# Hybrid S5 and attention trunk: first transfers reordered and merged, ScalarE's input squares and sines moved behind the split of the seventh weight unit

## The chip, the cores and the metric

The kernel runs on one core of a Trainium2 chip. The metric is the device time of one execution in microseconds (us); lower is better. The core has five engines that run side by side and meet through semaphores: TensorE (PE, its weight loads are called PEld), VectorE (DVE), ScalarE (ACT), GpSimd (POOL) and SyncE (SP), which here only issues transfers (DMAs).

## The reference

The input is `x`, 256 tokens of 1024 channels. There are two layers, each of the form

```
h = h + 0.5 * swiglu(rmsnorm(h), ffn1)
h = h + mixer(rmsnorm(h))         # layer 0: S5 state space + GLU; layer 1: MoBA attention
h = h + 0.5 * swiglu(rmsnorm(h), ffn2)
```

and a last rmsnorm. `swiglu` multiplies by a 1024 x 5632 matrix, takes silu(g) * u, and multiplies by a 2816 x 1024 matrix. `rmsnorm` needs for each token the mean of its squares; because the gain is folded into the matmul's input, the factor 1/rms of a token (the kernel's `rs`) can be applied to the matmul's result. The S5 mixer needs, for each of 64 groups with 64 states, `exp(a_re*dt)`, `cos(a_im*dt)`, `sin(a_im*dt)` with `dt = exp(log_step)`, and from them matrices built of `b_re`, `b_im`, `c_re`, `c_im` and powers of the decay. All is float32.

## The kernel before, in words

Each float32 matmul is done as three matmuls of rounded parts: hi*hi, lo*hi and hi*lo. So the weights have to be split on the way. A *unit* is 128 x 1024 weights (512 KB). SP loads units in order into six buffers `raw` (`load`, L294). ACT copies one into its rounded high part `w_hi` (`split`, L539 to L546). DVE subtracts to get the low part `w_lo` (L779 to L785). PE then runs twelve 512-column matmuls on it (`unit`, L1108). `w_hi` and `w_lo` have four buffers, so ACT may be four units ahead of PE. Units are counted from 0 here; the seventh is unit 6.

Phase 0 is the first half of the first swiglu: eleven blocks of four units each. Block 0 is units 0 to 3, block 1 is units 4 to 7. Each block fills two PSUM banks (one for 128 tokens each). Then ACT applies silu with the scale `rs` (`gate`, L555), DVE multiplies by u (`gated`, L813, tile `prod`), and PE transposes `prod` (`turn_hidden`, L1055). PE has the transposes of block b-1 in its program behind the second unit of block b: for block 0 they stand behind unit 5 and ahead of unit 6, and they wait for DVE's `drained`. ACT's `gate` of block 0 waits for `rs_ready`, which POOL raises once it has the mean squares (`inverse_rms`, L363, waits for `sq_done`).

Every engine works through its own program in order. ACT's program at the start is: the rounded input `x_hi` in eight tiles, with the splits of units 0 to 2 in between (L650 to L660); the exponential of `log_step` (L662); four squares of the input `h` with a sum each (L664 to L671), which wait for the two transfers of `h`; then `dense(0)`, whose loop splits unit j+3 at step j of block 0, and behind the split at j = 1 (unit 4) does the S5 angles (`s5_angles`, L637: one Exp, two Sin); at the next block it does `gate` of block 0 and goes on with the split of unit 7.

SP's program is at first: `xt` in four parts with units 0 to 3 in turn; the two halves of `h`; `skip`, `b_re`, `b_im`, `c_re`, `c_im`; then all other units from 4 on. From unit 6 on a load waits until the buffer is free (L297). ACT issues the small transfers: `gains`, `a_re`, `a_im`, and `log_step` in two.

POOL prepares the S5 tables meanwhile (L387 to L465): it computes the angle, waits for the squares (L403), for `b` and `c` (L404), and for ACT's three angle results (L409), and then works through a long chain of small operations on `sm`, `w2`, `cp`, `rotc` and `rots`. It needs to be done when PE has finished phase 1, since its next work (`w2_bd`, L477, the first step of the S5 mixer) waits for that (L468).

Of the kernel before, what the change touches and what calls it, by code (L numbers as in the profile page):

```python
# [12 lines left out]
ACT = mybir.ActivationFunctionType  # L13
# [4 lines left out]
P = 128  # L18
TOK = 256
TT = TOK // P  # L20
D = 1024
DT = D // P
# [9 lines left out]
S5_G, S5_J, S5_N = 64, 16, 64  # L32
GP = S5_G // 2
# [5 lines left out]
NB = 512  # L39
# [3 lines left out]
RAW = 6  # L43
# [51 lines left out]
def trunk(nc, io, out):  # L95
    phases = plan()
    units = [(p, v) for p in phases for v in range(p.units)]
# [4 lines left out]
    def sb(name, shape, dt=F32, where=None):  # L102
        return (where or ctx).enter_context(nc.sbuf_tensor(name, shape, dt))

    def sem(name):
        return ctx.enter_context(nc.semaphore(name))

    with ctx:
# [5 lines left out]
        h = sb("h", [P, TT, D])  # L114
        prod = sb("prod", [P, 2, TT, HB])
        act_out = sb("act_out", [P, TT, HB])
        ident = sb("ident", [P, P])
        gains = sb("gains", [P, 7, DT])
        skip = sb("skip", [P, DT])
        half = sb("half", [P, 2])  # L120
        nhalf = sb("nhalf", [P, 2])
        eye = sb("eye", [P, 32])
        ss = sb("ss", [P, TT, 4])
# [29 lines left out]
        with ExitStack() as area:  # L153
            w2 = sb("w2", [P, 2, STEP, GP, S5_J], F32, area)
# [3 lines left out]
            sm = sb("sm", [P, SMALLS, GP], F32, area)  # L158
            u = sb("u", [P, DT, TOK], F32, area)
            with ExitStack() as inner:  # L160
                tmp = sb("tmp", [P, 4, GP * S5_J], F32, inner)
# [4 lines left out]
            states = sb("states", [P, 2, PPT, 2, CH], F32, area)  # L166
# [42 lines left out]
        h_in = [sem(f"h_in{q}") for q in range(TT)]  # L209
        par_in = sem("par_in")  # L210
        s5_a_in = sem("s5_a_in")
        s5_in = sem("s5_in")
        consts = sem("consts")
        warm = sem("warm")
        low_first = sem("low_first")
        high_first = sem("high_first")
        sq_done = sem("sq_done")
# [74 lines left out]
        @block.sync  # L292
        def _(sp):
            def load(gu):  # L294
                p, v = units[gu]
                if gu >= RAW:
                    sp.wait_ge(lo_done, gu - RAW + 1)  # L297
                b, j = divmod(v, p.upb)
                if gu == 0:
                    for i in range(KU):  # L300
                        cols = slice(NB * i, NB * i + NB)
                        sp.dma_start(raw[:, 0, cols], io[WEIGHTS[p.n]][b, :, cols])\
                          .then_inc(first_in[i], 16)
                    return
                sp.dma_start(raw[:, gu % RAW, :], io[WEIGHTS[p.n]][b, :, j * UW:j * UW + UW])\
                  .then_inc(landed[gu % RAW], 16)

            for c in range(DT // 2):
                sp.dma_start(xt[:, 2 * c:2 * c + 2, :], io["xt"][:, 2 * c:2 * c + 2, :])\
                  .then_inc(x_in[c], 16)  # L310
                load(c)
            for q in range(TT):
                sp.dma_start(h[:, q, :], io["x"][q, :, :]).then_inc(h_in[q], 16)
            sp.dma_start(skip[:, :], io["skip"]).then_inc(s5_in, 16)
            for r, name in ((0, "b_re"), (1, "b_im")):
                sp.dma_start(tmp[:, r, :], io[name]).then_inc(s5_in, 16)
            for r, name in ((0, "c_re"), (1, "c_im")):
                sp.dma_start(w2[:, r, 0, :, :].rearrange("p g j -> p (g j)"), io[name])\
                  .then_inc(s5_in, 16)
            for gu in range(DT // 2, len(units)):  # L320
                load(gu)
            for q in range(TT):
                for ready, cols in ((left_ready, slice(0, NB)), (right_ready, slice(NB, D))):
                    sp.wait_ge(ready, q + 1)
                    sp.dma_start(out[q, :, cols], fin[:, q, cols]).then_inc(out_sent, 16)
            sp.wait_ge(out_sent, 16 * 2 * TT)

        @block.gpsimd
        def _(pool):
# [30 lines left out]
            def ts(o, a, s1, s2, op0=ALU.mult, op1=ALU.add):  # L360
                link(pool.tensor_scalar(o, a, s1, s2, op0, op1))
# [13 lines left out]
            def s(i):  # L375
                return sm[:, i, :]
# [7 lines left out]
                tt(o_i, t1, t2, ALU.add)  # L384

            ts(nhalf[:, :], half[:, :], -1.0, 0.0)
            pool.wait_ge(s5_a_in, 16 * 4)  # L387
            ts(s(A_RE), s(A_RE), -1e-4, 0.0, ALU.min, ALU.add)
            pool.wait_ge(s5_exp, 1)
            tt(s(XA), s(A_RE), s(DTM), ALU.mult)  # L390
# [10 lines left out]
            pool.tensor_scalar(s(RR), s(RR), PI_LOW, -PI_LOW, ALU.min, ALU.max)\  # L401
                .then_inc(s5_small, 1)
            inverse_rms(None)  # L403
            pool.wait_ge(s5_in, 16 * 5)  # L404

            for r in range(2):
                link(pool.tensor_scalar(cp[:, r, :, 0, :],
# [61 lines left out]
            for d in range(DT):  # L469
                b = d % 2  # L470
# [54 lines left out]

        @block.scalar
        def _(act):
            act.dma_start(gains[:, :, :], io["gains"]).then_inc(par_in, 16)
            act.wait_ge(consts, 1)
            act.activation(act_out[:, 0, 0:TT], mhalf[:, :], ACT.Copy).then_inc(warm, 1)  # L530
            act.dma_start(sm[:, 0, :], io["a_re"]).then_inc(s5_a_in, 16)
            act.dma_start(sm[:, 1, :], io["a_im"]).then_inc(s5_a_in, 16)
            for g in range(2):
                act.dma_start(sm[64 * g:64 * g + 64, 2, :],
                              io["log_step"][g:g + 1, :].broadcast_to([64, GP])).then_inc(s5_a_in, 16)

            tally = {"sq": 2 * TT}

# [86 lines left out]
            def dense(n, chained=True):  # L625
                p = phases[n]
                for b in range(p.blocks):
                    for j in range(p.upb):
                        if b:
                            after(p, b - 1, j)  # L630
                        elif chained:
                            after(phases[n - 1], phases[n - 1].blocks - 1, j)
                        split(p.unit0 + b * p.upb + j + LEAD)
                        if n == 0 and b == 0 and j == 1:
                            s5_angles()

            def s5_angles():  # L637
                act.wait_ge(s5_small, 1)
                act.activation(sm[:, 9, :], sm[:, 4, :], ACT.Exp).then_inc(s5_exp, 1)
                act.activation(sm[:, 10, :], sm[:, 7, :], ACT.Sin).then_inc(s5_exp, 1)  # L640
                act.activation(sm[:, 11, :], sm[:, 7, :], ACT.Sin, scale=0.5).then_inc(s5_exp, 1)
# [8 lines left out]
            for d in range(DT):  # L650
# [7 lines left out]
                    split(1)  # L658
                if d == 5:
                    split(2)  # L660
            act.wait_ge(s5_a_in, 16 * 4)
            act.activation(sm[:, 3, :], sm[:, 2, :], ACT.Exp).then_inc(s5_exp, 1)  # L662
            act.wait_ge(warm, 1)
            for q in range(TT):  # L664
                act.wait_ge(h_in[q], 16)
                for c in range(2):
                    if q or c:
                        act.wait_ge(sq_done, 2 * q + c)
                    act.activation(act_out[:, :, :].rearrange("p q x -> p (q x)"),  # L669
                                   h[:, q, NB * c:NB * c + NB], ACT.Square,  # L670
                                   accum_out=ss[:, q, c:c + 1]).then_inc(sq_done, 1)  # L671
            dense(0, False)
            dense(1)
            squares(phases[1], 1, NB)

# [708 lines left out]
```

## Time and profile before

| what | us |
|---|---|
| median of 3 timed runs (lowest, highest) | 1003.34 (1002.96, 1005.39) |
| profiled execution | 1005.62 |
| its span, first to last instruction | 1003.8 |
| PE busy | 976.4 (97%) |
| DVE busy | 596.8 (59%) |
| ACT busy | 485.1 (48%) |
| POOL busy | 238.2 (24%) |

The busy time of an engine leaves out waits, so an engine at 97% is the one that sets the time as long as its idle pieces are not on a path of others. The profile's tables give a start in us from the span's start, a duration, the engine, the line of the kernel and the tile written and read; in brackets stands how long the engine was idle before and what ended it. TensorE's granted clock is shown as a share of full speed: 1.00 is 2.4 GHz and 0.50 is 1.2 GHz.

### The profile page before, as it was taken

To read this page: it belongs to the slowest core of one execution; us is meant where nothing else is said; L and a number is where in the kernel's file an instruction comes from. 1 tells how busy PE (TensorE), PEld (TensorE's weight loads), DVE (VectorE), ACT (ScalarE), POOL (GpSimd) and SP (SyncE) were. 2 spreads that over 40 slices of the span, in tenths; PEclk is the share of its full clock that TensorE was granted. 3 is DMA by queue.
4 is the path that set the end of the run, shared out by engine and by line. 5 is a ranking of instruction groups with operands and counts; after the bars stand their busy time and mean duration, and the time that the engine had idled before them with its cause. 6 is when DMAs were issued, how large, how long until landed. Compare 5 with 4: busy or idle time off the path is not lost.

```text
span 1003.8 us, 14476 instructions
## 1 busy us (share of the span) xinstructions
PE 976.4 (97%) x5754; PEld 808.7 (81%) x5754; DVE 596.8 (59%) x732; ACT 485.1 (48%) x688; POOL 238.2 (24%) x307
## 2 busy tenths in 40 slices
PE   7999999888899999999999999999999999999997
PEld 6888888777788888888888888888887788888886
DVE  4767755859766555554565555554566465555544
ACT  6544444423265544544463444543457464444442
POOL 4999989779300000000000000000050000000000
PEclk9999999959999999999999999999999999999999
DMA  9766666600056566666656666666661256566651
GB/s 339 232 187 187 187 191 182 197 2 4 23 173 191 186 186 188 190 195 185 202 176 188 189 186 183 187 182 195 184 184 62 86 172 187 186 188 189 184 173 42
DMA packets 48035, 169.33 MB, mean 169 GB/s; under 512 B 5984, under 2 KB 5984, under 8 KB 47968
## 3 DMA queue, kind: packets, MB, share of 16 engines
q1 hardware_dynamic: 47232, 167.80, 55.0%
q8 instruction: 46, 0.75, 0.3%
q10 hardware_dynamic: 736, 0.60, 0.2%
q14 instruction: 21, 0.17, 0.1%
HBM read 167.33 MB, written 1.05 MB: 168 GB/s over the span
## 4 chain that ended last, share of the span: by engine, by line
PE 92%; POOL 2%; DVE 2%; issue 1%; ACT 1%; DMA 1%; SPq 0%; POOLq 0%; DVEq 0%; ACTq 0%
PE ps L1053 88%; PE ps L1064 2%; POOL w_bd L477 1%; DMA h<-in_x 1%; PE ps L1077 1%; PE ps L1194 1%; POOL c_bd L488 1%; PE ps L1286 1%; PE ps L1090 0%; PE ps L1258 0%; DVE scan L968 0%; ACT act_out L669 0%; ACT w_hi L545 0%; POOL decay L495 0%; PE ps L1313 0%
## 5 line engine op out<-in xcount | busy, mean ns | idle before, releaser
L783 DVE TENSOR_TENSOR w_lo<-raw,w_hi 128x1024 fp32r<-128x1024 f32 x311 | 406.1, 1309 | 276.3 <-ACT w_hi L545 275.7
L545 ACT ACTIVATE w_hi<-raw 128x1024 fp32r<-128x1024 f32 x311 | 328.4, 1058 | 274.0 <-PE ps L1053 271.7
L1053 PE MATMUL ps<-w_hi,x_hi 128*128 128x512 f32 x896 | 355.6, 397 | 4.3 <-DVE w_lo L783 4.2
L1053 PE MATMUL ps<-w_hi,x_lo 128*128 128x512 f32 x896 | 350.2, 391 | 0.0
L1053 PE MATMUL ps<-w_lo,x_hi 128*128 128x512 f32 x896 | 349.7, 390 | 0.0
L1053 PEld LDWEIGHTS ps<-w_hi,x_hi 128*128 128x128 f32 x896 | 169.0, 189 | 39.5 <-DVE w_lo L783 5.0
L1053 PEld LDWEIGHTS ps<-w_hi,x_lo 128*128 128x128 f32 x896 | 168.7, 188 | 36.1
L1053 PEld LDWEIGHTS ps<-w_lo,x_hi 128*128 128x128 f32 x896 | 169.2, 189 | 33.6
L1053 PE MATMUL ps<-w_hi,hid_hi 128*128 128x512 f32 x352 | 137.6, 391 | 0.0
L1053 PE MATMUL ps<-w_hi,hid_lo 128*128 128x512 f32 x352 | 137.0, 389 | 0.0
L1053 PE MATMUL ps<-w_lo,hid_hi 128*128 128x512 f32 x352 | 137.0, 389 | 0.0
L358 POOL TENSOR_TENSOR ms<-ss 128x2 f32<-128x2 f32 x6 | 1.2, 200 | 536.0 <-ACT act_out L583 535.5
L1053 PEld LDWEIGHTS ps<-w_hi,hid_lo 128*128 128x128 f32 x352 | 66.1, 188 | 13.8
L1053 PEld LDWEIGHTS ps<-w_lo,hid_hi 128*128 128x128 f32 x352 | 66.1, 188 | 13.6
L1053 PEld LDWEIGHTS ps<-w_hi,hid_hi 128*128 128x128 f32 x352 | 66.1, 188 | 13.5
L574 ACT ACTIVATE hid_hi<-ps 128x512 fp32r<-128x512 f32 x44 | 26.3, 599 | 88.0 <-PE ps L1064 88.0
L834 DVE TENSOR_TENSOR hid_lo<-ps,hid_hi 128x512 fp32r<-128x512 f32 x44 | 30.4, 692 | 57.1 <-ACT hid_hi L574 57.1
L565 ACT ACTIVATE act_out<-ps,rs 128x256 f32<-128x256 f32 x88 | 41.5, 475 | 46.2 <-PE ps L1053 46.1
L821 DVE SCALAR_TENSOR_TENSOR prod<-ps,rs,act_out 128x256 f32<-128x256 f32 x88 | 41.8, 480 | 18.0 <-ACT act_out L565 18.0
L523 POOL TENSOR_TENSOR rs<-end_ms,mhalf 128x1 f32<-128x1 f32 x2 | 1.1, 553 | 183.7 <-DVE end_ms L1042 183.7
L358 POOL TENSOR_TENSOR sm<-sm 128x32 f32<-128x32 f32 x64 | 34.3, 535 | 10.5 <-ACT sm L662 3.9
L358 POOL TENSOR_TENSOR tmp<-cp,sm 128x512 f32<-128x512 f32 x16 | 26.7, 1666 | 1.3
(129 smaller groups left out, 664.6 us busy)
## 6 DMA issues: line engine op xcount, KB each, us to landing
raw<-in_in SPq DMA_DIRECT2D x175, 512.0 KB, 4.1
raw<-in_out SPq DMA_DIRECT2D x88, 512.0 KB, 3.6
raw<-in_glu SPq DMA_DIRECT2D x16, 512.0 KB, 3.8
raw<-in_k SPq DMA_DIRECT2D x8, 512.0 KB, 4.5
raw<-in_v SPq DMA_DIRECT2D x8, 512.0 KB, 4.4
raw<-in_q SPq DMA_DIRECT2D x8, 512.0 KB, 4.3
raw<-in_o SPq DMA_DIRECT2D x8, 512.0 KB, 4.1
xt<-in_xt SPq DMA_DIRECT2D x4, 256.0 KB, 6.1
```

The source lines that it names most:

```text
L358: link(pool.tensor_tensor(o, a, b, op))
L477: pool.tensor_scalar(w2_bd[:, b, r, :, :, cols], w2[:, r, :, PPT * d:PPT * d + PPT, :], half[:, g:g + 1], 0.0, ALU.mult, ALU.add).then_inc ...
L488: pool.tensor_scalar(c_bd[:, d % 3, r, :, :, cols], cp[:, r, PPT * d:PPT * d + PPT, :, :], (half, nhalf)[r][:, g:g + 1], 0.0, ALU.mult, AL ...
L545: act.activation(w_hi[:, gu % WS, :], raw[:, gu % RAW, :], ACT.Copy)\
L565: act.activation(act_out[:, q, :], ps[:, bank(p.block0 + b, q), 0:HB], ACT.Silu, scale=rs[:, q:q + 1]).then_inc(act_ready, 1)
L574: act.activation(hid_hi[:, 2 * b:2 * b + 2, :].rearrange("p f x -> p (f x)"), ps[:, KT + hb % 2, :], ACT.Copy).then_inc(hid_hi_done, 1)
L783: dve.tensor_tensor(w_lo[:, gu % WS, :], raw[:, gu % RAW, :], w_hi[:, gu % WS, :].bitcast(F32), ALU.subtract)\
L821: dve.scalar_tensor_tensor(prod[:, hb % 2, q, :], ps[:, bank(gb, q), HB:NB], rs[:, q:q + 1], act_out[:, q, :], ALU.mult, ALU.mult).then_in ...
L834: dve.tensor_tensor(hid_lo[:, 2 * b:2 * b + 2, :].rearrange("p f x -> p (f x)"), ps[:, KT + hb % 2, :], hid_hi[:, 2 * b:2 * b + 2, :].rear ...
L1053: return pe.matmul(o, w, x, start=start, stop=stop, skip_group_check=True)
L1064: last = pe.transpose(ps[:, KT + hb % 2, f * TOK + q * P:f * TOK + q * P + P], prod[:, hb % 2, q, f * P:f * P + P], ident[:, :])
L1077: last = pe.transpose(ps[:, TA + t % 2, i * TOK + q * P:i * TOK + q * P + P], h[:, q, d * P:d * P + P], ident[:, :])
```

## The change

SP's order of transfers becomes: `xt` and units 0 to 3 as before, unit 4, the two halves of `h`, unit 5, `b` (both parts in one transfer), `c` (both in one), unit 6 and so on. `skip` travels with `gains` in one transfer on ACT's queue; `a_re`, `a_im` and `log_step` (now repeated for every state in the input) come in one transfer `a_step` in place of four. On ACT the four squares of the input leave their place ahead of `dense(0)` and the angles leave theirs behind the split of unit 4; both now stand behind the split of unit 6, squares first, and so directly ahead of `gate` of block 0.

```diff
-        gains = sb("gains", [P, 7, DT])
-        skip = sb("skip", [P, DT])
+        gains_skip = sb("gains_skip", [P, 8 * DT])
+        gains = gains_skip[:, 0:7 * DT].rearrange("p (n d) -> p n d", d=DT)
+        skip = gains_skip[:, 7 * DT:8 * DT]
...
                 load(c)
+            load(4)
             for q in range(TT):
                 sp.dma_start(h[:, q, :], io["x"][q, :, :]).then_inc(h_in[q], 16)
-            sp.dma_start(skip[:, :], io["skip"]).then_inc(s5_in, 16)
-            for r, name in ((0, "b_re"), (1, "b_im")):
-                sp.dma_start(tmp[:, r, :], io[name]).then_inc(s5_in, 16)
-            for r, name in ((0, "c_re"), (1, "c_im")):
-                sp.dma_start(w2[:, r, 0, :, :].rearrange("p g j -> p (g j)"), io[name])\
-                  .then_inc(s5_in, 16)
-            for gu in range(DT // 2, len(units)):
+            load(5)
+            sp.dma_start(tmp[:, 0:2, :].rearrange("p r x -> p (r x)"), io["b"]).then_inc(s5_in, 16)
+            sp.dma_start(w2[:, :, 0, :, :].rearrange("p r g j -> p r (g j)"),
+                         io["c"].rearrange("p (r x) -> p r x", r=2)).then_inc(s5_in, 16)
+            for gu in range(RAW, len(units)):
                 load(gu)
...
-            act.dma_start(gains[:, :, :], io["gains"]).then_inc(par_in, 16)
+            act.dma_start(gains_skip[:, :], io["gains_skip"]).then_inc(par_in, 16)
             act.wait_ge(consts, 1)
             act.activation(act_out[:, 0, 0:TT], mhalf[:, :], ACT.Copy).then_inc(warm, 1)
-            act.dma_start(sm[:, 0, :], io["a_re"]).then_inc(s5_a_in, 16)
-            act.dma_start(sm[:, 1, :], io["a_im"]).then_inc(s5_a_in, 16)
-            for g in range(2):
-                act.dma_start(sm[64 * g:64 * g + 64, 2, :],
-                              io["log_step"][g:g + 1, :].broadcast_to([64, GP])).then_inc(s5_a_in, 16)
+            act.dma_start(sm[:, 0:3, :].rearrange("p n g -> p (n g)"), io["a_step"]).then_inc(s5_a_in, 16)
...
                         split(p.unit0 + b * p.upb + j + LEAD)
-                        if n == 0 and b == 0 and j == 1:
+                        if n == 0 and b == 0 and j == 3:
+                            input_squares()
                             s5_angles()
+
+            def input_squares():
+                act.wait_ge(warm, 1)
+                for q in range(TT):
+                    act.wait_ge(h_in[q], 16)
+                    for c in range(2):
+                        if q or c:
+                            act.wait_ge(sq_done, 2 * q + c)
+                        act.activation(act_out[:, :, :].rearrange("p q x -> p (q x)"),
+                                       h[:, q, NB * c:NB * c + NB], ACT.Square,
+                                       accum_out=ss[:, q, c:c + 1]).then_inc(sq_done, 1)
...
             act.activation(sm[:, 3, :], sm[:, 2, :], ACT.Exp).then_inc(s5_exp, 1)
-            act.wait_ge(warm, 1)
-            for q in range(TT):
-                act.wait_ge(h_in[q], 16)
-                for c in range(2):
-                    if q or c:
-                        act.wait_ge(sq_done, 2 * q + c)
-                    act.activation(act_out[:, :, :].rearrange("p q x -> p (q x)"),
-                                   h[:, q, NB * c:NB * c + NB], ACT.Square,
-                                   accum_out=ss[:, q, c:c + 1]).then_inc(sq_done, 1)
             dense(0, False)
```

The waits on `s5_a_in` and `s5_in` are lowered to the new numbers of transfers. Nothing that is computed changes.

## Rows read from the trace of the kernel before

**Rows 1.** The page, busy shares and the chain that ended last, by engine:

```profile
PE 976.4 (97%) x5754; PEld 808.7 (81%) x5754; DVE 596.8 (59%) x732; ACT 485.1 (48%) x688; POOL 238.2 (24%) x307
PE 92%; POOL 2%; DVE 2%; issue 1%; ACT 1%; DMA 1%; SPq 0%; POOLq 0%; DVEq 0%; ACTq 0%
```

**Rows 2.** Timeline of PE: start, duration, what, [idle before, releaser]:

```profile
17.10 0.39 PE L1053 MATMUL ps<-w_hi,x_lo 128*128 128x512 f32 x1
19.88 0.50 PE L1053 MATMUL ps<-w_hi,x_hi 128*128 128x512 f32 x1 [2.39 <-DVE w_lo L783]
...
28.19 0.60 PE L1064 MATMUL ps<-ident,prod 128*128 128x128 f32 x4
...
266.87 1.29 PE L1053 MATMUL ps<-u,k_t 32*32 32x256 f32 x32 [3.64 <-DVE k_t L988]
```

**Rows 3.** Timeline of ACT at the start:

```profile
13.08 0.21 ACT L662 ACTIVATE sm<-sm 128x32 f32<-128x32 f32 x1
14.57 0.63 ACT L669 ACTIVATE act_out<-h 128x512 f32<-128x512 f32 x1 [1.27 <-DMA h<-in_x]
...
17.52 1.04 ACT L545 ACTIVATE w_hi<-raw 128x1024 fp32r<-128x1024 f32 x1
19.73 1.06 ACT L545 ACTIVATE w_hi<-raw 128x1024 fp32r<-128x1024 f32 x1 [1.17 <-DMA raw<-in_in]
20.70 0.21 ACT L639 ACTIVATE sm<-sm 128x32 f32<-128x32 f32 x1
20.93 1.28 ACT L640 ACT_TABLE_LOAD   x1
...
22.48 1.99 ACT L545 ACTIVATE w_hi<-raw 128x1024 fp32r<-128x1024 f32 x2
24.49 1.28 ACT L565 ACT_TABLE_LOAD   x1
25.78 0.84 ACT L565 ACTIVATE act_out<-ps,rs 128x256 f32<-128x256 f32 x2
```

**Rows 4.** Timeline of DVE at the start:

```profile
18.60 1.23 DVE L783 TENSOR_TENSOR w_lo<-raw,w_hi 128x1024 fp32r<-128x1024 f32 x1 [4.17 <-ACT w_hi L545]
...
26.29 0.88 DVE L821 SCALAR_TENSOR_TENSOR prod<-ps,rs,act_out 128x256 f32<-128x256 f32 x2 [0.32 <-ACT act_out L565]
```

**Rows 5.** Chain of waits, 0 to 32 us, one piece (start, us):

```profile
5.50 8.98 DMA h<-in_x
```

**Rows 6.** SP's issues of units 3 and 6 (timeline), and their us to landing:

```profile
4.78 0.69 SPq L305 DMA_DIRECT2D raw<-in_in  x1
raw<-in_in SPq DMA_DIRECT2D x1, 512.0 KB, 8.4
11.09 1.07 SPq L305 DMA_DIRECT2D raw<-in_in  x1
raw<-in_in SPq DMA_DIRECT2D x1, 512.0 KB, 11.2
```

**Rows 7.** DMA queues in 0 to 14 us, ACT's queue: packets, MB, share of 16 engines:

```profile
q10 hardware_dynamic: 592, 0.08, 3.5%
```

**Rows 8.** Timeline of POOL:

```profile
18.98 2.02 POOL L407 TENSOR_SCALAR cp<-w 128x512 f32<-128x512 f32 x2
22.71 0.24 POOL L358 TENSOR_TENSOR sm<-sm 128x32 f32<-128x32 f32 x1 [1.71 <-ACT sm L641]
...
187.33 3.27 POOL L358 TENSOR_TENSOR rots<-tmp 128x1024 f32<-128x1024 f32 x1
197.05 1.84 POOL L477 TENSOR_SCALAR w_bd<-w,half 128x256 f32<-128x256 f32 x4 [6.46 <-PE ps L1053]
```

**Rows 9.** Stretches: length, busy PE, PEld, DVE, ACT, POOL, PEclk, DMA, GB/s:

```profile
17.50:19.90 2.40, 0.02 (x1) 0.03 (x1) 1.23 (x1) 1.23 (x4) 2.03 (x4) 1.00 1.03 421
268.00:270.00 2.00, 2.00 (x76) 1.75 (x66) 0.00 (x0) 0.11 (x1) 0.00 (x0) 0.58 0.00 0
270.00:272.00 2.00, 2.00 (x6) 1.57 (x7) 0.72 (x2) 1.64 (x3) 0.00 (x0) 0.57 0.04 8
```

More of the change, by code:

```diff
@@ L386, in _ @@
             ts(nhalf[:, :], half[:, :], -1.0, 0.0)
-            pool.wait_ge(s5_a_in, 16 * 4)
+            pool.wait_ge(s5_a_in, 16)
             ts(s(A_RE), s(A_RE), -1e-4, 0.0, ALU.min, ALU.add)
@@ L403, in _ @@
             inverse_rms(None)
-            pool.wait_ge(s5_in, 16 * 5)
+            pool.wait_ge(s5_in, 16 * 2)
             for r in range(2):
@@ L660, in _ @@
                     split(2)
-            act.wait_ge(s5_a_in, 16 * 4)
+            act.wait_ge(s5_a_in, 16)
             act.activation(sm[:, 3, :], sm[:, 2, :], ACT.Exp).then_inc(s5_exp, 1)
-            act.wait_ge(warm, 1)
-            for q in range(TT):
-                act.wait_ge(h_in[q], 16)
-                for c in range(2):
-                    if q or c:
-                        act.wait_ge(sq_done, 2 * q + c)
-                    act.activation(act_out[:, :, :].rearrange("p q x -> p (q x)"),
-                                   h[:, q, NB * c:NB * c + NB], ACT.Square,
-                                   accum_out=ss[:, q, c:c + 1]).then_inc(sq_done, 1)
             dense(0, False)
@@ L1357 @@
         "xt": _np.ascontiguousarray(x["x"][0].T.reshape(DT, P, TOK).transpose(1, 0, 2)),
-        "gains": tiles(_np.stack([x["ffn1_norm"][0], x["mix_norm"][0], x["ffn2_norm"][0],
-                                  x["kv_norm"], x["ffn1_norm"][1], x["mix_norm"][1],
-                                  x["ffn2_norm"][1]])),
+        "gains_skip": _np.ascontiguousarray(tiles(_np.stack([
+            x["ffn1_norm"][0], x["mix_norm"][0], x["ffn2_norm"][0], x["kv_norm"], x["ffn1_norm"][1],
+            x["mix_norm"][1], x["ffn2_norm"][1], x["s5_d"][0]])).reshape(P, -1)),
         "last_gain": _np.ascontiguousarray(x["final_norm"].reshape(1, D)),
-        "skip": tiles(x["s5_d"][0]),
-        "a_re": states(x["s5_a_re"][0]), "a_im": states(x["s5_a_im"][0]),
-        "log_step": _np.ascontiguousarray(x["s5_log_step"][0].reshape(GP, 2).T),
-        "b_re": states(x["s5_b_re"][0]), "b_im": states(x["s5_b_im"][0]),
-        "c_re": states(x["s5_c_re"][0].transpose(0, 2, 1)),
-        "c_im": states(x["s5_c_im"][0].transpose(0, 2, 1)),
+        "a_step": _np.concatenate([states(x["s5_a_re"][0]), states(x["s5_a_im"][0]),
+                                   states(_np.repeat(x["s5_log_step"][0][:, None], S5_N, 1))], 1),
+        "b": _np.concatenate([states(x["s5_b_re"][0]), states(x["s5_b_im"][0])], 1),
+        "c": _np.concatenate([states(x["s5_c_re"][0].transpose(0, 2, 1)),
+                              states(x["s5_c_im"][0].transpose(0, 2, 1))], 1),
         "glu": stream(x["s5_w_glu"][0], True),
```

## Prediction

> **What bounds the kernel now.** I read the page first. PE is busy 97% of the span and makes up 92% of the chain that ended last [rows 1]. So the question for an edit at the start is only: at what time does PE get through its first units, and does anything behind that give time back or take more? The timeline of PE answers the first half. Unit 2's last matmul starts at 17.10, and matmuls follow each other every 0.227 us, so unit 3 could start at 17.33; it starts at 19.88, 2.55 us later [rows 2]. The brackets name DVE's low part of unit 3, which starts at 18.60 behind ACT's high part at 17.52 [rows 3, 4]. ACT had been free from 13.29 on, but its program put the four squares of the input first, and these waited until 14.57 for the first half of `h` [rows 3]; the chain of waits shows the same transfer, 5.50 to 14.48 [rows 5]. Unit 3 itself had landed at 4.78 + 8.4 = 13.2 [rows 6]. From 19.88 on PE shows no idle time up to the transposes of block 0: units 3, 4 and 5 at 2.73 us each (12 x 0.227) give 28.1, and the transposes stand at 28.19 [rows 2]. They need DVE's `prod`, which was ready at 26.29 + 0.88 = 27.17 [rows 4]: a cover of 1.0 us only. That is the number on which the prediction turns.
>
> The second half is POOL. Its S5 tables end at 187.33 + 3.27 = 190.60, and it then waits 6.46 us for PE to finish phase 1 at about 197.0 [rows 8].
>
> **The change part by part.**
>
> *Squares out of the way of unit 3: a gain at first.* ACT can split unit 3 at 13.3, DVE has its low part before 16, so unit 3 starts at 17.33: PE is 2.55 us early. Unit 4, loaded ahead of `h`, takes the place in which `h` landed (14.5), and is ready before PE's 20.1. Unit 5 comes three transfers of 512 KB later. The rate: from `h` at 14.48 to unit 6 at 11.09 + 11.2 = 22.3 [rows 5, 6] the queue carries six times 512 KB (half of `h`, `b`, `c`, units 4, 5, 6), 1.30 us each. So unit 5 lands at 18.4, is split by 20.8, and PE wants it at 22.8. PE would end unit 5 at 17.33 + 3 x 2.73 = 25.5, against 28.1 before.
>
> *What is late next: the gate of block 0.* The order of transfers ahead of unit 6 changes, their bytes do not, so unit 6 lands at 22.3 again. Before, ACT had done the squares and the angles while it waited for transfers. Now they stand between unit 6's split and the gate. From durations in [rows 3]:
> - split of unit 6 to the next instruction: 0.97 (19.73 to 20.70);
> - four squares: 2.95 (14.57 to 17.52);
> - Exp, table load, two Sin: 1.78 (20.70 to 22.48);
> - table load for silu: 1.29 (24.49 to 25.78);
> - first silu to the end of the second `prod` on DVE: 27.17 - 25.78 = 1.39 [rows 3, 4].
>
> The sum is 8.38, and 0.1 for the semaphore to PE. From 22.3 the transposes of block 0 would start at 30.8. POOL's `rs` is not later than the silu table: 1.46 us behind the squares (17.52 to 18.98 [rows 3, 8]), less than the 3.07 of angles and table load. So PE, through with unit 5 at 25.5, waits over 4.5 us for the transposes, and unit 6 is queued behind them on PE. Instead of 2.55 us early PE is 2.6 us late against 28.19.
>
> *Fewer transfers.* ACT's small transfers took 3.5% of the 16 engines over 14 us, 0.49 us [rows 7]. Of 592 packets some 256 remain, so about 0.3 us is saved, and `skip`'s 128 packets save perhaps 0.1 more at the same rate. Bounds: 0 (they were interleaved with issue gaps) and 1.0 (twice the whole of ACT's queue). I take 0.4: unit 6 at 21.9, transposes at 30.4, PE 2.2 us late. The waits for `s5_a_in` end earlier on POOL, which waits for Exp at 13.08 anyway: nothing.
>
> The Trainium skill has a rule that speaks for this part: "DMA: Bandwidth & Descriptors", Bandwidth, says that transfers under 64 KB are dominated by their descriptors. The trace bounds what that is worth here by the 0.49 us above.
>
> *The clock.* An idle stretch of nearly 5 us (25.5 to 30.4) is new. In this trace PE was idle for 3.64 us up to 266.87 [rows 2], ran on, and from about 268.3 to 271.7 its granted clock was 0.5 (0.58 and 0.57 over two stretches of 2 us): PE lost 0.42 x 2 + 0.43 x 2 = 1.7 us there [rows 9]. The shorter gap at 17.5 to 19.9 kept 1.00 [rows 9]. The new gap is longer than either. Bounds: 0, if the clock stays or falls and rises within the gap, and 3.4, two such stretches. I take 1.4: one stretch of half clock whose first part falls in the idle time.
>
> *POOL.* Its chain started at 22.71 behind ACT's sines. Now: squares end, `rs`, the two copies of 2.02, then the chain. Squares end at 21.9 + 0.97 + 2.95 = 25.8; `rs` and copies +1.46 and +2.1: 29.4. The chain is 6.7 us later and ends at 197.3, if its operations take what they took (I allow +-2). PE ends phase 1 at 197.0 + 2.2 + 1.4 = 200.6. POOL is covered by 3 us, and costs nothing; the cover before was 6.46 [rows 8].
>
> *Behind that.* All later phases follow PE's end of phase 1, so nothing gives the time back. `w_hi` buffers, loads and the gate of block 1 are as before, shifted.
>
> **Sum.** -2.55 (unit 3 earlier) + 4.75 (wait for the transposes, net +2.2) + 1.4 (clock) = +3.6 us. Against the profiled execution (span 1003.8, whole 1005.62) that is 1009.2. The timed runs' median is 2.3 us under the profiled one, so the forecast is 1003.34 + 3.6 = 1006.9. What a measurement can tell from no change is 0.3%, 3.0 us: 1000.3 to 1006.35.
>
> **The rivals.**
> 1. *The clock stays up* (it did over the gap of 2.4 us). Then +2.2: 1005.5, within 0.3%. Against it: three microseconds of idle and more were followed by half clock at 268. Chance 0.17.
> 2. *The other side: the gate is not late.* If unit 6 is at ACT long before 21.9 (by 17.0, were the transfers faster at the start), or ACT gets through the list above inside PE's units 4 and 5, PE keeps 2.55 us and is at the end of phase 1 at 194.5. Then POOL decides: its chain ends at 197.3 when the sines stay where the diff has them, the S5 stage starts at 197.3 in place of 197.05, and the result is +0.3: 1003.6. If POOL's chain has less contention or starts sooner, it lies between that and -2.55, 1000.8; only beyond that is it faster by 0.3%. It decides from the point where `prod` of block 0 is ready by 28.2. For it: nothing but errors in my landing times; against it: unit 6's bytes are the same. Chance 0.15, of which 0.05 is faster than 1000.3.
> 3. *The clock takes two stretches,* or half clock comes again in S5 by another alignment: +2.2 + 3.1 = +5.3, 1008.6. Chance 0.13.
> 4. *Table loads cost more than their row when they stand close together:* ScalarE would have to empty first. In [rows 3] the load of 1.28 starts 0.02 behind the Exp and the silu 0.01 behind its load, so I see no such time; with one more 1.4 us on each of two loads, +2.8 on the forecast: 1009.7. Chance 0.03. The Trainium skill says this ("ScalarE: Activation LUTs", What ACT_TABLE_LOAD costs: a drain of some 1.38 us beside the load of 1.28). The trace agrees on the 1.28 and shows no drain.
>
> The forecast itself has 0.52. Its own spread (unit 6's landing +-0.6, clock 0.7 to 1.7) is 1005.6 to 1007.8.
>
> **How the numbers follow.** Slower than 1006.35: two thirds to three quarters of the forecast (0.38), rivals 3 and 4 (0.15), and a little of rival 1 by the scatter of medians (0.02): 0.55. Faster: 0.06. The rest, 0.39, within 0.3%. The range from 1003.3 (rival 2's +0.3, less a little scatter) to 1009.0 leaves out the faster part of rival 2, rival 4 and half of the tail of 3, together under 0.2.
>
> **What would show it.** Unit 3's first matmul at about 17.3 with no idle time before it: the first gain is right. Unit 4 landed at about 14.5, unit 6 at 21.9. ACT in the order split 6, four squares, Exp, two table loads with the sines between, silu from about 29.0. PE idle for 4 to 5 us ahead of L1064 released by DVE's `prod`: the central step. PEclk under 1 at 30 to 33: the clock term; 1.00 there: rival 1. POOL's idle time before L477 near 3 us; if it is 0, rival 2 or a longer POOL chain. The prediction is wrong if the transposes of block 0 start before 28.2, or if ACT's squares are done before unit 6 is split.

## The result, and the profile after

The change made the kernel slower. Five runs of each gave medians of 1008.95 us (1006.21 to 1012.15) and 1002.96 us (1001.87 to 1005.39) for the kernel before, with a ratio of 1.0064, 95% interval 1.0038 to 1.0090. In a later session twelve runs of the same changed kernel stood against 35 of the kernel before: 1006.47 and 1003.62, ratio 1.0028, interval 1.0010 to 1.0047. By the ends of the two intervals the change costs 1 to 9 us, and the forecast of +3.6 lies in between. The direction and the mechanism were right. One term was too small, the landing of unit 6, and the spread of single runs was larger than I had allowed for. Both are read from the profiles below.

The timeline of PE after the change, the rows that answer to [rows 2]:

```profile
24.69 0.39 PE L1052 MATMUL ps<-w_hi,x_lo 128*128 128x512 f32 x1
32.25 1.12 PE L1063 MATMUL ps<-ident,prod 128*128 128x128 f32 x4 [7.17 <-DVE prod L820]
...
45.05 0.60 PE L1063 MATMUL ps<-ident,prod 128*128 128x128 f32 x4
```

No idle time stands before unit 3 any more: PE is through unit 5 at 25.1, 3 us earlier than before. Then it waits 7.17 us for `prod` of block 0, and the transposes stand at 32.25 in place of 28.19. The next ones follow 12.80 us later; in the kernel before, blocks without a disturbance are 11.36 us apart. The difference of 1.4 us is the clock, which stands at half for a part of it (rows below).

ACT and DVE, answering to [rows 3, 4]:

```profile
13.40 1.04 ACT L541 ACTIVATE w_hi<-raw 128x1024 fp32r<-128x1024 f32 x1
14.69 1.06 ACT L541 ACTIVATE w_hi<-raw 128x1024 fp32r<-128x1024 f32 x1 [0.24 <-DMA raw<-in_in]
18.47 1.06 ACT L541 ACTIVATE w_hi<-raw 128x1024 fp32r<-128x1024 f32 x1 [2.72 <-DMA raw<-in_in]
23.73 1.06 ACT L541 ACTIVATE w_hi<-raw 128x1024 fp32r<-128x1024 f32 x1 [4.20 <-DMA raw<-in_in]
24.70 0.61 ACT L641 ACTIVATE act_out<-h 128x512 f32<-128x512 f32 x1
...
27.63 0.21 ACT L647 ACTIVATE sm<-sm 128x32 f32<-128x32 f32 x1
27.86 1.28 ACT L648 ACT_TABLE_LOAD   x1
...
29.52 1.28 ACT L561 ACT_TABLE_LOAD   x1
30.82 0.84 ACT L561 ACTIVATE act_out<-ps,rs 128x256 f32<-128x256 f32 x2
```

```profile
31.32 0.88 DVE L820 SCALAR_TENSOR_TENSOR prod<-ps,rs,act_out 128x256 f32<-128x256 f32 x2 [5.28 <-ACT act_out L561]
```

ACT stands idle for 2.72 and for 4.20 us while it waits for units 5 and 6, with the four squares and the angles still undone; then it does them ahead of the gate. From unit 6's landing to the transposes it takes 32.25 - 23.75 = 8.50 us; the sum in the prediction had 8.48.

Unit 6 is where the size went wrong. SP's issue and its us to landing, answering to [rows 6]:

```profile
9.05 0.68 SPq L306 DMA_DIRECT2D raw<-in_in  x1
raw<-in_in SPq DMA_DIRECT2D x1, 512.0 KB, 14.7
```

It landed at 9.05 + 14.7 = 23.75. (The view gives the second number to 0.1, so a landing is good to 0.05 us; ACT's split of unit 6 starts at 23.73.) The prediction took 21.9 and bounded it by 21.3 and 22.3. The transfers ahead of it came at its pace of one per 1.3 us: unit 4 at 14.7, the halves of `h` at 15.9 and 17.2, unit 5 at 18.4, `b` at 19.5, `c` at 21.0. One more step of 1.3 would have put unit 6 at 22.3. So the loss lies between `c` and unit 6, and there the DMA view shows a packet of another queue, called instruction, which is not in the same stretch of the kernel before. First the four transfers from unit 5's landing to unit 7's in the changed kernel, then the four behind `c_im` up to unit 7 in the kernel before:

```profile
q1 hardware_dynamic: 807, 2.61, 102.4%
q8 instruction: 1, 0.02, 1.1%
```

```profile
q1 hardware_dynamic: 579, 2.11, 102.5%
```

The packet carries 16 KB and takes one of the 16 DMA engines for 1.1 us, beginning at 21.56. The four transfers took 6.4 us with it and 5.1 without. The queues together moved 411 GB/s in both stretches, which fits one engine's share of a unit that comes late, and not a slower stream. In the kernel before such a packet begins at 25.2, behind unit 6's landing. The section on why the prediction was right or wrong has the other profiles.

The clock (busy us of PE, PEld, DVE, ACT, POOL, then PEclk, DMA share, GB/s), and POOL, answering to [rows 8, 9]:

```profile
28.43:35.26 6.83, 3.01 (x9) 2.57 (x10) 3.50 (x5) 6.51 (x10) 5.93 (x13) 0.50 0.19 53
28.00:32.00 4.00, 0.00 (x0) 0.00 (x0) 0.68 (x2) 3.96 (x7) 3.33 (x9) 0.55 0.27 111
32.00:36.00 4.00, 3.75 (x13) 3.15 (x14) 3.56 (x5) 2.98 (x4) 3.52 (x7) 0.59 0.23 51
```

The clock is at half for 6.83 us. The first 3.8 of them fall in PE's wait, 3.0 behind the transposes, and these cost the 1.4 to 1.5 us.

```profile
202.54 1.86 POOL L477 TENSOR_SCALAR w_bd<-w,half 128x256 f32<-128x256 f32 x4 [4.50 <-PE ps L1052]
```

POOL is still idle for 4.50 us when phase 1 ends (6.46 before), so its later start costs nothing. Phase 1 ends 202.54 - 197.05 = 5.5 us later, and the span is 5.9 us longer (1009.7).

### The profile page after: what moved, and what is told of

Read it like the earlier page. It is cut to its first block, busy times and chain, and to the rows that moved or that the text cites. A ratio compares the mean times of both kernels' runs of the same rounds, so it can differ in the third digit from the quotient of the medians.

```text
span 1009.7 us, 14470 instructions
## 1 busy us (share of the span) xinstructions
PE 978.1 (97%) x5754; PEld 809.6 (80%) x5754; DVE 594.3 (59%) x732; ACT 485.1 (48%) x688; POOL 240.8 (24%) x307
## 4 chain that ended last, share of the span: by engine, by line
PE 91%; DVE 2%; POOL 2%; issue 1%; DMA 1%; ACT 1%; SPq 1%; POOLq 0%; DVEq 0%; ACTq 0%
PE ps L1052 86%; PE ps L1063 2%; DMA raw<-in_in 1%; POOL w_bd L477 1%; PE ps L1076 1%; PE ps L1285 1%; PE ps L1193 1%; POOL c_bd L488 0%; DVE scan L967 0%; PE ps L1089 0%; PE ps L1257 0%; ACT act_out L641 0%; SPq L306 0%; DVE rot_b L974 0%; DVE rot_a L955 0%
## 5 line engine op out<-in xcount | busy, mean ns | idle before, releaser
L1052 PEld LDWEIGHTS ps<-w_lo,hid_hi 128*128 128x128 f32 x352 | 66.1, 188 | 13.6
L833 DVE TENSOR_TENSOR hid_lo<-ps,hid_hi 128x512 fp32r<-128x512 f32 x44 | 30.4, 692 | 57.6 <-ACT hid_hi L570 57.6
L1063 PE MATMUL ps<-ident,prod 128*128 128x128 f32 x176 | 26.8, 275 | 7.2 <-DVE prod L820 7.2
```

The lines of the kernel that those rows point to most:

```text
L833: dve.tensor_tensor(hid_lo[:, 2 * b:2 * b + 2, :].rearrange("p f x -> p (f x)"), ps[:, KT + hb % 2, :], hid_hi[:, 2 * b:2 * b + 2, :].rear ...
L1052: return pe.matmul(o, w, x, start=start, stop=stop, skip_group_check=True)
L1063: last = pe.transpose(ps[:, KT + hb % 2, f * TOK + q * P:f * TOK + q * P + P], prod[:, hb % 2, q, f * P:f * P + P], ident[:, :])
```

## The experiments

All changes are against the changed kernel unless another is named. With up to twelve runs against 35 or 23 of the kernel before, an interval is about +-0.2%, so 2 us; the stages of the profiles tell more than the times. In each profile I read four points: unit 6's landing, the transposes of block 0, POOL's first `w_bd` (the end of phase 1), and the first 512-column matmul of the GLU (the end of the S5 stage).

**e1_again**: the changed kernel as it is.

> The changed kernel once more. Theory A (the gate of block 0 stands behind unit 6's split, so PE waits for it): again an idle stretch of PE ahead of the transposes of block 0 (7.17 us before), transposes near 32 us, +5 to +7 us in time. What is open is why unit 6 landed at 23.75 and not at the 22.3 that the bytes ahead of it give. Rival A1 (its late landing comes from the order or form of the transfers): it lands at 23.5 to 24.0 again. Rival A2 (chance of this one execution): it lands at 22.0 to 22.5 and the transposes stand at 30.8.

Measured: 1006.47, ratio 1.0028 (1.0010 to 1.0047). Unit 6 landed at 22.69, and the transposes came 8.55 us later, with half clock behind them again:

```profile
31.24 1.12 PE L1063 MATMUL ps<-ident,prod 128*128 128x128 f32 x4 [5.85 <-DVE prod L820]
44.16 0.60 PE L1063 MATMUL ps<-ident,prod 128*128 128x128 f32 x4
```

So the same kernel has unit 6 at different times. Neither rival's number fits exactly; 22.69 is nearer to A2. In this profile it is unit 7 that came late, 2.3 us behind unit 6.

**e2_bc_four**: `b` and `c` as four transfers.

```diff
-            sp.dma_start(tmp[:, 0:2, :].rearrange("p r x -> p (r x)"), io["b"]).then_inc(s5_in, 16)
+            for r in range(2):
+                sp.dma_start(tmp[:, r, :], io["b"][:, NB * r:NB * r + NB]).then_inc(s5_in, 16)
...                       # c in the same way
```

> The changed kernel, but b and c are sent as four transfers of 256 KB again in place of two of 512 KB; order and all else stay. If the merged form of b or c makes unit 6 late: unit 6 lands at 22.3, transposes of block 0 at 30.8, time 1.4 us less than e1_again. If the form has no part in it: unit 6 at 23.75 as in e1_again, same time.

Measured: 1005.86, ratio 1.0032 (1.0013 to 1.0051). Unit 6 landed at 22.02, transposes at 30.61. The time does not differ from e1_again's, and e1_again shows the merged form with unit 6 at 22.69, so this run doesn't condemn the form. In e12_after_third below, with the merged form, unit 6 landed at 22.3.

**e3_act_only**: the kernel before with ScalarE's new order alone.

```diff
                         split(p.unit0 + b * p.upb + j + LEAD)
-                        if n == 0 and b == 0 and j == 1:
+                        if n == 0 and b == 0 and j == 3:
+                            input_squares()
                             s5_angles()
```

> All transfers as in the kernel before; only ScalarE's squares and angles stand behind unit 6's split. Theory A: unit 3 starts at 17.3, unit 6 lands at 22.3, transposes of block 0 at 22.3 + 8.5 = 30.8 (before 28.2), half clock behind the gap for 1.4 us: +4.0 us, 1007. Rival (the transfers, not ScalarE's order, cost the time): no change against before, 1003.

Measured: 1005.13, ratio 1.0018 (0.9999 to 1.0037). The gate went as forecast, to the tenth: unit 6's split starts at 22.29, transposes at 30.83, half clock behind them, phase 1 ends at 201.34. PE's wait has two parts here, though: with the old transfers unit 4 comes only at 19.7, PE waits 1.89 us for it, and 2.99 us for `prod`:

```profile
22.10 0.50 PE L1056 MATMUL ps<-w_hi,x_hi 128*128 128x512 f32 x1 [1.89 <-DVE w_lo L786]
30.83 0.66 PE L1067 MATMUL ps<-ident,prod 128*128 128x128 f32 x4 [2.99 <-DVE prod L824]
```

The time rose by 1.5 (interval 0 to 3.7), not 4.0: the S5 stage of this profile took 71.49 us against 72.71. That was the first sign that the later stages are not a constant.

**e4_dma_only**: the new transfers with ScalarE's old order.

```diff
-                        if n == 0 and b == 0 and j == 3:
-                            input_squares()
+                        if n == 0 and b == 0 and j == 1:
                             s5_angles()
...
             act.activation(sm[:, 3, :], sm[:, 2, :], ACT.Exp).then_inc(s5_exp, 1)
+            ...                # the four squares here again
```

> The new transfers alone; ScalarE's squares ahead of unit 3's split and the angles behind unit 4's, as in the kernel before. Theory A: the squares now wait for h until 15.9 and 17.2, unit 3 starts near 21.0 in place of 19.88, the gate of block 0 is in time for the transposes (29.2): +1.0 us, and up to 1.4 more if the gap ahead of unit 3 (16.7 to 21) lowers the clock: 1004 to 1005.5. Rival (the transfers carry the loss): +5 us or more, 1008.

Measured: 1005.93, ratio 1.0020 (0.9999 to 1.0042). The squares wait for `h` until 15.28, unit 3 starts at 20.59:

```profile
20.59 0.50 PE L1060 MATMUL ps<-w_hi,x_hi 128*128 128x512 f32 x1 [3.84 <-DVE w_lo L790]
30.53 0.60 PE L1071 MATMUL ps<-ident,prod 128*128 128x128 f32 x4
```

The transposes follow unit 5 without idle time, so the gate is in time, but a gap of 3.84 us and half clock behind it bring them to 30.53; phase 1 ends at 199.39. The time, +2.3 us (0 to 4.2), is within theory A's +1.0 to +2.4, and its transposes at 29.2 were missed by the clock. Each half of the change alone is slower at the start: transfers ordered for the new ScalarE order are late for the old one.

**e5_early**: the changed kernel with the squares behind unit 4's split and the angles behind unit 5's.

```diff
-                        if n == 0 and b == 0 and j == 3:
+                        if n == 0 and b == 0 and j == 1:
                             input_squares()
+                        if n == 0 and b == 0 and j == 2:
                             s5_angles()
```

> The changed kernel with the squares behind unit 4's split and the angles behind unit 5's, transfers as in the change. Theory A (what stands between unit 6's split and the gate is the cost): the gate needs only the silu table after unit 6's split; transposes of block 0 at 26 to 27 (e1_again: 31.24), no half clock, phase 1 ends near 195.5 (e1_again 201.7, before 197.05), POOL's tables done at 191; time 2 us under the kernel before. Rival (the change loses elsewhere, by its transfers or later stages): the transposes move but the time stays at +3.

Measured: 1000.28, ratio 0.9974 (0.9952 to 0.9995). Here unit 6 was late (23.73), yet the transposes stood at 27.58, 3.85 us behind it:

```profile
27.58 0.80 PE L1064 MATMUL ps<-ident,prod 128*128 128x128 f32 x4 [2.51 <-DVE prod L821]
40.59 0.60 PE L1064 MATMUL ps<-ident,prod 128*128 128x128 f32 x4
```

The gap of 2.51 us was followed by half clock all the same (13.01 us between the two), so phase 1 ended at 198.08 and not at 195.5. The wait for `prod` is smaller, as theory A has it; its 195.5 and its "no half clock" were missed. The timed runs are 0.5 to 4.8 us faster than the kernel before, but this profile does not show that at the start (198.08, against 197.05 and 198.79 in the two profiles of the kernel before): it is short by its S5 stage of 68.69 us. How much of the gain in time is the start's is not shown.

**e6_early_u6**: as e5_early, with unit 6 sent ahead of `b` and `c` (`load(6)` ahead of the two, the loop from `RAW + 1`).

> As e5_early, and unit 6 is sent ahead of b and c. Theory A: unit 6 lands at 20.3, is split at 21.8 behind the angles, transposes of block 0 at 25.5, phase 1 ends at 194.5, POOL (c lands at 22.5) is done at 192.5; time 2.5 to 3 us under the kernel before. Rival: POOL's chain is later than phase 1's end, then POOL shows no idle time ahead of w_bd L477 and the gain is smaller.

Measured: 1000.11, ratio 0.9955 (0.9935 to 0.9976): faster than the kernel before, by 2.4 to 6.5 us. ACT never waits for unit 6, and PE does not wait for `prod`:

```profile
21.25 1.05 ACT L542 ACTIVATE w_hi<-raw 128x1024 fp32r<-128x1024 f32 x1
22.31 1.28 ACT L562 ACT_TABLE_LOAD   x1
23.61 0.84 ACT L562 ACTIVATE act_out<-ps,rs 128x256 f32<-128x256 f32 x2
```

```profile
25.17 0.60 PE L1065 MATMUL ps<-ident,prod 128*128 128x128 f32 x4
36.52 0.60 PE L1065 MATMUL ps<-ident,prod 128*128 128x128 f32 x4
```

The distance is 11.35, so no half clock; phase 1 ends at 194.01, 3.0 us before [rows 8]. POOL's cover is down to 1.49 us there. Some of the gain is lost again right behind it: PE's first two waits in the S5 stage, for POOL's `w_bd` and DVE's `hn`, are 2.68 and 2.20 us, against 2.08 and 1.62 before. Why is open; e8_angles_late, where POOL's cover is 1.18 us, has 3.00 and 2.20.

**e7_fill** and **e10_fill24**: 14 and 24 matmuls of the identity on PE in its wait (the profile counts two for each, 28 and 48).

```diff
+                if p.n == 0 and b == 0 and j == 1:
+                    for i in range(FILL):
+                        mm(ps[:, TB, 0:P], ident[:, :], ident[:, :], True, True)
                 if p.name == "in" and j == 1:
                     turn_hidden(p, b)
```

> The changed kernel with 14 more 128x128 matmuls of the identity on PE (result not used) between unit 5 and the transposes of block 0; they fill some 5 of the 6 us in which PE waits. If the granted clock falls because of the gap: it stays at 1.00 from 25 to 45, and the two transposes (block 0 and block 1) are 11.4 us apart in place of 12.9; phase 1 ends 1.5 us earlier than in e1_again. If the clock falls for another reason: 12.9 again.

> As e7_fill with 24 matmuls in place of 14 (there 14 took 3.3 us at 0.235 us each, 2.3 us were left idle, and the clock fell all the same). 24 take 5.6 us and leave 0 to 1.7 us idle. If the gap lowers the clock: PEclk 1.00 from 25 to 45 in the profile and 11.4 us from the transposes of block 0 to those of block 1 (e1_again 12.9), time 1.5 us under e1_again. If the clock falls for another reason: 12.9 again.

Measured: 1006.40, ratio 1.0025 (1.0005 to 1.0045), and 1006.08, ratio 1.0012 (0.9990 to 1.0034). Both missed. 14 took 3.29 us and left 2.30 us idle ahead of the transposes, and these were 13.04 us apart. With 24 unit 6 was late (23.87), and 1.94 us stayed idle; PE in the wait and after it:

```profile
24.98 5.52 PE L1053 MATMUL ps<-ident 128*128 128x128 f32 x48
32.45 0.66 PE L1064 MATMUL ps<-ident,prod 128*128 128x128 f32 x4 [1.94 <-DVE prod L821]
...
31.00:34.00 3.00, 1.55 (x9) 1.38 (x10) 2.05 (x4) 2.99 (x5) 2.51 (x7) 0.98 0.00 0
34.00:37.00 3.00, 3.00 (x9) 2.32 (x8) 2.98 (x4) 1.17 (x2) 2.77 (x4) 0.50 0.60 171
```

The clock fell to 0.5 all the same, and the transposes were 13.00 us apart. So these two don't separate the gap from another cause: a wait of 1.94 us was left, and it may have been enough, as 2.51 was in e5_early.

**e8_angles_late**: the angles moved on, behind unit 8's split (`if n == 0 and b == 1 and j == 1`).

> The changed kernel with only the angles moved on, behind unit 8's split and so behind the gate of block 0. Theory A: one table load and 1.8 us go out from ahead of the gate, POOL's rs becomes the last to come; transposes of block 0 at 29.0 to 29.5 (e1_again 31.24), PE 2 us earlier. POOL's chain starts only near 34.5, ends near 202, and decides the start of the S5 stage: no idle time on POOL ahead of w_bd L477, which starts at 201.5 to 203; time equal to e1_again or 1 us more. If POOL had room to spare instead: w_bd at 199.5 and the time 2 us under e1_again.

Measured: 1008.81, ratio 1.0051 (1.0026 to 1.0075). Unit 6 was late (23.36). ACT:

```profile
28.84 1.28 ACT L561 ACT_TABLE_LOAD   x1 [1.44 <-POOL rs L370]
30.13 0.84 ACT L561 ACTIVATE act_out<-ps,rs 128x256 f32<-128x256 f32 x2
...
32.88 1.28 ACT L648 ACT_TABLE_LOAD   x1
34.17 0.23 ACT L648 ACTIVATE sm<-sm 128x32 f32<-128x32 f32 x1
34.42 1.28 ACT L649 ACT_TABLE_LOAD   x1
```

The transposes came 8.21 us behind unit 6's landing; the expected 29.0 to 29.5 were 6.3 to 6.8 us behind e1_again's landing at 22.69. The silu table load stands behind the wait for POOL's `rs`, so 1.46 and 1.29 add up where I had let them overlap. Exp, left alone behind silu, costs a further table load. POOL's chain ended at 202.1, as expected, and `w_bd` began at 203.29 with 1.18 us idle. So the expectation that POOL decides was missed: PE still decides, by a little.

**e9_squares_early**: the squares alone moved back, behind unit 4's split.

> The changed kernel with the squares alone moved back, behind unit 4's split; the angles stay behind unit 6's. Theory A by its sum: from unit 6's landing to the transposes of block 0 it takes 8.5 - 2.95 = 5.55 us (0.97 split, 1.78 angles, 1.29 silu table, 1.39 silu and prod, 0.1): 27.6 if unit 6 lands at 22.0, 29.3 if at 23.7, against PE's 25.1. Idle of PE 2.5 to 4.2 us, phase 1 ends 197.5 to 200, time about that of the kernel before, 1 to 3 us less than e1_again. If it were the angles' table load and not the squares that made the gate late: no change against e1_again.

Measured: 1002.41, ratio 0.9986 (0.9964 to 1.0008). Unit 6 landed at 22.49, transposes at 28.12, 5.63 us behind (expected 5.55):

```profile
28.12 0.66 PE L1064 MATMUL ps<-ident,prod 128*128 128x128 f32 x4 [2.92 <-DVE prod L821]
39.54 0.60 PE L1064 MATMUL ps<-ident,prod 128*128 128x128 f32 x4
```

A gap of 2.92 us, and here the distance is 11.42: the clock stayed up, the only one of the ten profiles with an idle wait ahead of these transposes where it did. Phase 1 ends at 197.03, as in the kernel before.

**e11_before_again** and **e12_after_third**: one more profile of each kernel.

> The kernel before once more, for its stages: phase 1 ends at 197 (+-1); the S5 stage (72.7 us in its first profile) takes 68 to 75 us by how many stretches of half clock fall in it. If the stage takes 72.7 again the spread of single times must come from elsewhere.

> The changed kernel a third time. Unit 6 landed at 23.75, 22.69 (and 21.6 to 23.8 in kernels with the same transfers). Transposes of block 0 at its landing + 8.5, end of phase 1 at 201 to 203, S5 stage anywhere in 68 to 75.

Measured: single times 1007.31 (before) and 1005.66 (changed), so in this pair the changed kernel was the faster one. The kernel before, second profile:

```profile
19.98 0.50 PE L1053 MATMUL ps<-w_hi,x_hi 128*128 128x512 f32 x1 [2.52 <-DVE w_lo L783]
29.93 0.60 PE L1064 MATMUL ps<-ident,prod 128*128 128x128 f32 x4
...
198.79 1.84 POOL L477 TENSOR_SCALAR w_bd<-w,half 128x256 f32<-128x256 f32 x4 [10.57 <-PE ps L1053]
```

```profile
17.50:21.00 3.50, 1.02 (x4) 0.89 (x5) 1.29 (x2) 2.33 (x5) 2.94 (x5) 0.97 1.03 415
21.00:24.50 3.50, 3.50 (x10) 2.68 (x10) 2.03 (x2) 3.47 (x6) 1.54 (x5) 0.54 1.03 410
```

Its gap ahead of unit 3, harmless in the first profile [rows 9], was followed by half clock here, and the transposes came at 29.93 in place of 28.19. My expectation of 72.7 us for the S5 stage as the sign of another cause came true for this kernel (72.69 in both profiles), but over all profiles the stage does spread. Stretches from the end of phase 1 to 5 us into the GLU, for the kernel before, the first profile after, and e12_after_third:

```profile
197.05:274.80 77.75, 65.21 (x1506) 55.11 (x1507) 55.03 (x95) 24.71 (x55) 53.88 (x91) 0.80 0.05 15
```

```profile
202.54:280.60 78.06, 65.71 (x1506) 55.52 (x1507) 54.84 (x95) 24.64 (x55) 55.69 (x91) 0.78 0.05 17
```

```profile
202.24:277.10 74.86, 60.17 (x1510) 50.64 (x1511) 57.73 (x96) 24.87 (x55) 57.56 (x91) 0.91 0.05 14
```

The last number but two is the granted clock. Twice its shortfall from 1.00 times the length gives the time at half clock: some 31, 34 and 13 us. The stages behind differ by one stretch of half clock, here in e11_before_again, and none in e12_after_third:

```profile
780.00:794.00 14.00, 12.38 (x78) 10.68 (x78) 5.93 (x16) 6.23 (x16) 0.00 (x0) 0.88 0.07 18
```

```profile
780.00:796.00 16.00, 14.37 (x92) 12.40 (x92) 7.42 (x16) 7.70 (x16) 0.00 (x0) 1.00 0.15 45
```

The table puts the profiles side by side (us; the last two columns are the S5 stage and the rest of the span behind it):

| profile | unit 6 landed | transposes | phase 1 ends | S5 | rest |
|---|---|---|---|---|---|
| before | 22.3 | 28.19 | 197.05 | 72.7 | 734.0 |
| e11_before_again | 22.4 | 29.93 | 198.79 | 72.7 | 734.0 |
| after | 23.75 | 32.25 | 202.54 | 73.1 | 734.1 |
| e1_again | 22.7 | 31.24 | 201.67 | 72.4 | 731.5 |
| e12_after_third | 22.3 | 30.81 | 202.24 | 69.8 | 731.6 |
| e3_act_only | 22.3 | 30.83 | 201.34 | 71.5 | 733.5 |
| e4_dma_only | 21.6 | 30.53 | 199.39 | 72.4 | 731.6 |
| e9_squares_early | 22.5 | 28.12 | 197.03 | 72.4 | 731.6 |
| e5_early | 23.7 | 27.58 | 198.08 | 68.7 | 731.6 |
| e6_early_u6 | not waited for | 25.17 | 194.01 | 71.1 | 733.5 |
| e2_bc_four | 22.0 | 30.61 | 201.19 | 74.3 | 733.4 |
| e7_fill | 21.8 | 30.38 | 200.90 | 74.3 | 733.4 |
| e10_fill24 | 23.9 | 32.45 | 202.94 | 69.9 | 731.5 |
| e8_angles_late | 23.4 | 31.57 | 203.29 | 74.6 | 734.0 |

At the start the changed kernel is later in all three profiles: 202.15 on average against 197.92, so +4.2 us. Behind it S5 takes 68.7 to 74.6, and the rest is either 731.5 to 731.6 or 733.4 to 734.1. Both go with the granted clock in all fourteen profiles. S5 takes 68.7 to 69.9 where some 13.6 us of it are at half clock, 71.1 and 71.5 with 19.3, 72.4 to 72.7 with 27.3 to 30.7, and 73.1 to 74.6 with 32.2 to 33.1. The rest is 733.4 or more in just the eight profiles that have half clock between 781 and 799. These two parts together differ by up to 8 us between profiles of kernels that are the same behind the start, and by 5.8 us between the three profiles of the changed kernel. The timed runs say the same without a profile: of 23 runs of the kernel before, the fastest has 1000.79 us at a mean granted clock of 0.993, the slowest 1009.76 at 0.977.

## Why the prediction was right or wrong

- *Unit 3 no longer waits for the squares.* Right: no idle time ahead of it, PE through unit 5 at 25.1 where the prediction had 25.5. With the new transfers unit 1 landed at 8.2 to 9.0 in place of 9.3 to 9.4; it bought nothing, since PE then waited longer for the transposes.
- *The gate of block 0 is late next.* Right, and shown from both sides: with the same transfers and the squares and angles earlier the idle time goes from 7.17 or 5.85 to 2.51 (e5_early) and to none (e6_early_u6); with the old transfers and ScalarE's new order alone it appears (e3_act_only). The sum of 8.48 us between unit 6's landing and the transposes measured 8.50, 8.55 and 8.51 in the changed kernel's three profiles; without the squares 5.63 (e9_squares_early).
- *Unit 6's landing.* This is the step that failed: a term of the sum that was mis-sized. The prediction took 21.9, bounds 21.3 and 22.3, because the bytes ahead of the unit and their rate do not change. It measured 23.75, 22.69 and 22.3 in the changed kernel. Of ten profiles with this order of transfers up to unit 6, six had it at 21.6 to 22.7 and four at 23.4 to 23.9; the three profiles with the old order had 22.3 to 22.4. Fewer transfers saved nothing to speak of. Constant bytes at a constant rate did not settle when a transfer lands: where unit 6 came at 23.75, unit 7 came 1.1 us behind it, and where it came at 22.69, unit 7 came 2.3 us behind.
- *What stands beside the late landings.* In nine of those ten profiles the instruction queue's packet begins between 21.2 and 21.9, and the four transfers from unit 5's landing to unit 7's take 5.4 to 6.6 us. In the tenth, e4_dma_only, it begins at 25.8 and they take 5.15. In the three with the old order it begins at 25.1 to 25.2, and four transfers up to unit 7 take 5.12. In e6_early_u6, where unit 6 is ahead of `b` and `c` and so ahead of the packet, the packet is there too, but at most 0.1 us is lost. So the bounds left out a packet of another queue, beside which unit 6 came 1.4 to 1.6 us late in four profiles, and unit 7 up to 1 us late in five. No run moved the packet alone, so that it is the cause is read from fourteen profiles and not tested. Open are why it comes 4 us sooner when both halves of the change are in (with ScalarE's order alone or the transfers alone it does not), and why unit 6 is the late one in some executions and unit 7 in others. The form of `c` and `b` (e2_bc_four) was not shown to matter.
- *The clock, 1.4 us.* Right in size in the kernel's three profiles: the distance of the transposes less 11.36 is 1.4, 1.6 and 2.6 (the last is e12_after_third, where the half clock began later in the wait and so had more of it behind the transposes). The picture behind the number was not right: the prediction had one stretch like the 3.4 us at 268, and the half clock lasted 6.8 us in all three. That 3.6 to 3.8 us of them fell in the wait in the first two, and left 1.4 and 1.6, is luck. That the kernel before can pay for its own gap of 2.5 us, as in e11_before_again (+1.7), I had not seen: one profile showed 1.00, and I took that for its nature. On these two profiles of the kernel before, it about halves what the clock adds to the difference (1.9 less 0.9).
- *Rivals 1 and 3.* Rival 1, that the clock stays up, came in no profile of the changed kernel. Rival 3 had 3.1 us for the clock, from two stretches or from half clock in S5 by another alignment. At the start e12_after_third comes near it with 2.6; in S5 and behind it the half clock did fall differently from one execution to the next, but in both directions; that the change has a part in it is not shown.
- *POOL is covered.* Right: 4.5 to 5.2 us idle ahead of `w_bd`, the prediction had 3. POOL's own chain varies, too: in the kernel before it ended at 190.60 in one profile and at 188.22 in the other. Rival 2, that the gate is in time and POOL decides, did not come; e6_early_u6 shows that the gate in time is worth 3 us at phase 1's end and that POOL would still have 1.49 us.
- *Rival 4, a drain beside each table load*, is out: 27.86 + 1.28 = 29.14, and Sin starts at 29.15; 29.52 + 1.28 = 30.80, silu at 30.82. The Trainium skill's figure for the load (ScalarE: Activation LUTs, What ACT_TABLE_LOAD costs) agrees with the 1.28; its drain does not show here.
- *"Behind that ... nothing gives the time back."* In the pair of profiles at the result this held: +5.5 us at the end of phase 1, +5.9 at the end. It failed for single runs, and with it the range: the later stages differ by up to 8 us between executions through the clock. That they neither return nor add time on average because of the change is not shown; the profiles are too few. So the first five runs gave +6.0 and twelve others +2.8. The five had a mean granted clock of 0.983, the twelve 0.986; by the kernel before's 9.0 us for 0.016 of clock (1000.79 to 1009.76), an estimate, 1.7 of the 2.5 us between the two medians go with that. A range built from the start's terms alone, with its top at 1009.0, sat right at the edge of what was measured. The ratio of 1.0064 would put the changed kernel at 1009.8 against the 1003.34 shown before, beyond that top.
- *Sum.* Forecast +3.6 (net 2.2 for the gate, 1.4 for the clock); at the end of phase 1 the profiles have +4.2 on average, +5.5 in the first pair. The excess of 1.9 in the first pair is unit 6, 1.85 us later than the 21.9. In the average it is smaller by luck of two errors against each other: unit 6 was later than forecast by 1.0 us, and the kernel before once paid for a gap itself. The sum's two parts do not quite follow from its own figures (25.5 to 30.4 is a wait of 4.9, not 4.75, and 25.5 is 2.7 ahead of 28.19), but the net 2.2 does.

## What to carry to other kernels

When work is moved out of the way of one wait, look at what its engine does at the new place: here ACT sat idle for 2.7 and 4.2 us at the splits of units 5 and 6 and then did 4.7 us of postponed work on the path of the gate. The place that gains is the idle stretch itself (e6_early_u6, by 2.4 to 6.5 us), and the transfer that ends the stretch has to be sent early enough. Before a change of a few us is priced, take more than one profile of the kernel before and compare by stages: two profiles of the same kernel differed by 1.7 us at the start alone. A landing that is computed from bytes and rate needs a bound for what other queues send in between.

## What was not expected of the hardware

- A gap on PE of 2.5 us was followed by a granted clock of 0.5 in some executions (e5_early 2.51, e11_before_again 2.52; each about 1.7 us lost) and not in others ([rows 9] 2.39, e9_squares_early 2.92). A fill of the gap with 128x128 matmuls of the identity down to 1.94 us did not keep it up (e10_fill24).
- One packet of 16 KB on another queue, 1.1 us of one DMA engine, stood beside a landing that came up to 1.6 us late, while the queues together kept moving 411 GB/s.
- A table load was held by the wait of the instruction behind it: in e8_angles_late it starts at 28.84 behind POOL's `rs`, with ACT idle for 1.44 us before. In the changed kernel `rs` is ready at 29.09 and the load starts at 29.52, so `rs` was 0.4 us from deciding there, too.
